# Eight row places instead of up to twelve for the expert rows of the first token block

## The reference, cut to what matters

```python
def peer_ffn(x, w_query, sub_keys, expert_down, expert_up):   # 2 blocks of 128 tokens
    q = (xb @ w_query).reshape(t, 8, 2, 64)
    s = einsum('thpd,hpkd->thpk', q, sub_keys)                # 8 heads, 2 x 128 keys
    top_s, top_i = top_k(s, 16)
    ...                                                       # best 16 of 16 x 16 pairs
    u = expert_down[idx]                                      # one row of 1024 a token and pick
    act = gelu(einsum('td,thkd->thk', xb, u))
    vv = expert_up[idx]
    return einsum('thk,thkd->td', gate * act, vv)
```

## Time and profile before

| | |
|---|---|
| median of 3 runs | 1270.54 us (1269.96 to 1271.0) |
| the profiled execution, own time | 1269.91 us |
| its span, first to last instruction | 1268.2 us |
| mean granted clock of TensorE | 0.98 |
| PE busy | 1172.7 us (92%) |
| DVE busy | 711.9 us (56%) |
| ACT busy | 622.5 us (49%) |
| POOL busy | 752.9 us (59%) |
| bytes by the gathers (queue 0) | 268.45 MB of 381.78 MB |

### The profile page before, as it was taken

One profiled execution on the slowest core, in us unless ns is written; L12 is line 12 of the kernel. 1 busy time (PEld: TensorE's weight loads), 2 busy tenths in 40 slices (PEclk: granted clock), 3 DMA queues, 4 the chain that ended last, 5 costly groups with the idle time before them and its releaser, 6 DMA issues.

```text
span 1268.2 us, 15414 instructions
## 1 busy us (share of the span) xinstructions
PE 1172.7 (92%) x5672; PEld 818.9 (65%) x5672; DVE 711.9 (56%) x1512; ACT 622.5 (49%) x1344; POOL 752.9 (59%) x481
## 2 busy tenths in 40 slices
PE   9999999999998677787799798889999999999998
PEld 8987999965553233333355353443599998888887
DVE  5443135399686675766859678665546533422223
ACT  8586555544434232234424553554654675544442
POOL 7696668645553344554444445454247678788885
PEclk9999999999999898889999999999999999999999
DMA  8553446999999999999999999999524446565542
GB/s 278 193 197 117 149 151 240 370 376 426 425 424 424 424 424 424 424 424 425 424 421 425 424 424 424 416 418 424 218 88 159 134 137 196 167 199 194 181 157 100
DMA packets 121996, 381.78 MB, mean 301 GB/s; under 512 B 8512, under 2 KB 66880, under 8 KB 89152
## 3 DMA queue, kind: packets, MB, share of 16 engines
q0 software_dynamic: 36864, 268.45, 50.7%
q1 hardware_dynamic: 83584, 112.25, 26.7%
q10 hardware_dynamic: 1472, 0.09, 0.1%
HBM read 379.72 MB, written 1.05 MB: 300 GB/s over the span
## 4 chain that ended last, share of the span: by engine, by line
PE 65%; DMA 20%; DVE 7%; ACT 4%; POOL 2%; issue 1%; ACTq 0%; DVEq 0%; POOLq 0%
DMA rows_w<-peer_rows_in,arena 17%; PE ps L1140 15%; PE ps L835 13%; PE ps L864 8%; PE ps L1391 6%; PE ps L1444 4%; PE ps L1395 3%; PE ps L1193 3%; DVE rows_w L2527 3%; PE ps L1344 2%; PE ps L1369 2%; POOL rows_w L778 1%; DMA arena<-peer_rows_in,arena 1%; PE ps L1214 1%; ACT wgt L1770 1%
## 5 line engine op out<-in xcount | busy, mean ns | idle before, releaser
L565 POOL TENSOR_TENSOR w_lo<-ring,w_hi 128x1024 fp32r<-128x1024 f32 x178 | 434.1, 2456 | 160.1 <-ACT w_hi L559 160.0
L1140 PE MATMUL ps<-rows_w,diag 128*128 128x512 f32 x672 | 324.5, 622 | 57.1 <-ACT diag L1779 57.1
L778 POOL DMA_INDIRECT rows_w<-peer_rows_in,arena x168 | 195.4, 1163 | 233.5 <-PE ps L1140 196.9
L1140 PEld LDWEIGHTS ps<-rows_w,diag 128*128 128x128 f32 x672 | 128.1, 199 | 220.4 <-issue 136.6
L2527 DVE CUSTOM_DVE_ANT_0 rows_w<-rows_w,arena 128x1024 f32<-128x1024 f32 x168 | 203.5, 1224 | 103.3 <-DMA rows_w<-peer_rows_in,arena 102.7
L559 ACT ACTIVATE w_hi<-ring 128x1024 fp32r<-128x1024 f32 x178 | 184.1, 1058 | 105.2 <-PE ps L1395 45.5
L1768 ACT ACTIVATE gelu<-dots,rr 128x4 f32<-128x4 f32 (+2 forms) x91 | 27.0, 296 | 318.6 <-DVE dots L2527 318.1
L1140 PE MATMUL ps<-arena,diag 128*128 128x512 f32 x260 | 124.3, 607 | 13.6 <-ACT diag L1779 13.5
L778 POOL DMA_INDIRECT arena<-peer_rows_in,arena x66 | 76.0, 1151 | 59.6 <-PE ps L1140 51.2
L2527 DVE CUSTOM_DVE_ANT_0 arena<-arena 128x1024 f32<-128x1024 f32 x66 | 80.5, 1224 | 37.8 <-DMA arena<-peer_rows_in,arena 37.6
L1140 PEld LDWEIGHTS ps<-arena,diag 128*128 128x128 f32 x260 | 48.5, 194 | 75.0 <-issue 54.1
(11 more groups left out here) (468 smaller groups left out, 2042.6 us busy)
## 6 DMA issues: line engine op xcount, KB each, us to landing
ring<-w_in_in SPq DMA_DIRECT2D x38, 1024.0 KB, 5.2
ring<-w_ffn_gate_in SPq DMA_DIRECT2D x11, 1024.0 KB, 5.3
ring<-w_ffn_up_in SPq DMA_DIRECT2D x11, 1024.0 KB, 5.3
ring<-w_ffn_down_in SPq DMA_DIRECT2D x11, 1024.0 KB, 4.9
ring<-w_out_in SPq DMA_DIRECT2D x8, 1024.0 KB, 7.2
ring<-w_branch_attn_in SPq DMA_DIRECT2D x4, 1024.0 KB, 5.3
ring<-w_branch_mlstm_in SPq DMA_DIRECT2D x4, 1024.0 KB, 5.2
arena<-w_in_in SPq DMA_DIRECT2D x2, 2048.0 KB, 12.1
```

What stands on the lines that cost most here:

```text
L565: pool.tensor_tensor(lo_of(n, u)[:, t, 0:cols], raw_half(n, g)[:, t, 0:cols], hi_of(n, u)[:, t, 0:cols].bitcast(F32), ALU.subtract).then_i ...
L778: pool.indirect_dma_start(pick_row(p, 0, 2 * D), None, a["peer_rows"], bass.IndirectOffsetOnAxis(ap=idx[:, g // PH, j:j + 1], axis=0)).the ...
L1140: ins = pe.matmul(acc[:, c, :], diag[:, p % 4, :], pick_row(p, D + c * CW, CW), start=(p == first), stop=True, skip_group_check=True)
```

## The change

The four places in the ring are added at picks 131, 134, 137 and 140 and no longer at 19, 26, 39 and 52. Up to pick 130 the gathers go round eight places. `TURN_OF_PLACES` grows from 64 to 160, and the swaps that lead to `LAST_PLACES` are made in picks 160 to 255, two passes in a turn and not one. The last turns are the same as before.

```diff
-NEW_AT = {19: 8, 26: 9, 39: 10, 52: 11}
-TURN_OF_PLACES = PICKS // 4
+NEW_AT = {131: 8, 134: 9, 137: 10, 140: 11}
+TURN_OF_PLACES = 160
...
 order = PLACE[-NS:]
 for turn in range((PICKS - TURN_OF_PLACES) // NS):
-    for i in range(turn % 2, NS - 1, 2):
+    for i in (*range(0, NS - 1, 2), *range(1, NS - 1, 2)):
         if LAST_PLACES.index(order[i]) > LAST_PLACES.index(order[i + 1]):
             order[i], order[i + 1] = order[i + 1], order[i]
```

## The result

| | before | after |
|---|---|---|
| median of 4 runs | 1270.45 us | 1289.55 us (1287.44 to 1291.52) |
| ratio, 95% interval | | 1.0148 (1.0136 to 1.0161) |
| the profiled execution, own time | 1269.91 us | 1289.23 us |
| its span | 1268.2 us | 1287.5 us |
| mean granted clock of TensorE | 0.98 | 0.97 |

The change makes the kernel 19.1 us slower. The prediction had the direction and the place, and a fifth of the size: 4.0 us, with a range that ended at 1281.0.

What follows compares the result with a forecast made beforehand. The DMA queue, never empty, was taken to set the pace from first pick to last. The profiled 1269.91 us, plus 4.0 for late groups in picks 64 to 130, plus 0.6 to the median, gave about 1274.4; range 1270.8 to 1281.

Steps and rivals of the forecast that it cites:

- Before pick 64: Stage with two dots at a time: eight places lose nothing, and removing the waits for `query_done` gains nothing.
- The landing into an empty queue: Picks 64 to 130: time from a gather instruction's end to its landing, taken as 5.4 us, between 4.67 and 6.86.
- The sum of a round: Picks 64 to 130, four dots at a time: an undisturbed group just closes, 0.05 us late; 4.0 us lost in all.
- seven long products of the trace before: Seven of 17 groups, picks 64 to 131, have slow first products; the longest cost 1.0 us twice, others 0.6 three times.
- rival 2: Picks 64 to 130: most groups miss through slower landings or fewer full-clock groups; 6.7 to 14 us lost, 1277 to 1285; chance 0.18.
- landings behind the first: Right behind an idle queue landings do not stay at pitch: the first two came 3.4 us apart, not 2.47.
- From pick 131: Four new places refill the queue by four picks, 10 us; block 1's shortest return, 10 picks or 24.7 us, loses nothing.
- What the profile after was to show: In 431 to 600 us: two to five stretches under 424 GB/s, issue to landing 6.5 to 10 us, some late first dots.
- the rate sags in block 1: Sign that would prove the prediction wrong; it expected 413 GB/s in block 1, as before.
- Rival 1: Picks 64 to 130: the loop of eight places closes and nothing changes; 1270.5 to 1272.5 us; chance 0.27.
- Rival 3: In the 1 MB steps a shallower gather queue moves more than 424 GB/s; up to 3 us gained, 1267.5; chance 0.05.
- Rival 4: Another wait than `row_free` holds POOL at eight places, such as unrouted row numbers; no cost, chance counted within Rival 1.

Runs made afterwards that it cites:

- run 1: The changed kernel plus empty TensorE products in idle time: 32 after pick 63, 12 after every fourth pick from 67 to 131; 1278.92 us, ratio 1.0076.
- run 2: The changed kernel plus only the 32 empty TensorE products after pick 63; 1290.05 us, ratio 1.0156.
- run 3: The kernel before the change plus the same empty TensorE products as in run 1; 1270.14 us, ratio 0.9997.
- run 9: The changed kernel with the four ring places added at picks 73 to 76, so one round alone is late; 1273.49 us, ratio 1.0022.
- run 10: The changed kernel with the ring places added at picks 97, 100, 103 and 106, so four late rounds, not eight; 1277.98 us, ratio 1.0058.
- run 5: The changed kernel with a ninth ring place added at pick 19, nine places up to pick 133; 1271.73 us, ratio 1.0010.
- run 14: The changed kernel with a ninth place from pick 19, the others at 136 to 138, one swap pass a turn; 1270.57 us, ratio 1.0002.

## Why the prediction was wrong

**What bounds the kernel, and how a loss comes about: right.** DMA sets the pace, POOL's long waits cost nothing until the queue runs dry, and what is lost stays lost. The prediction named the stage (fours with eight places), the chain (first product, gather, landing) and the first pick that would miss, 72.

**Before pick 64: right.** The landings are 0.7 us behind those of the trace before at pick 0 and 0.1 us ahead of them at pick 71, and 408 and 425 GB/s stand there; the removed waits for `query_done` brought nothing.

**The landing into an empty queue: right in the mean, in part by luck.** It was put at 5.4 us from the instruction's end; eight cases after give 4.5 to 6.9, mean 5.4. But the queue was not empty as at the first gather of all, which took 4.67: at the end of the instruction the gather before still had 0.35 to 1.8 us to its landing. The Trainium skill, page DMA: Bandwidth & Descriptors, section Anatomy of one DMA, would have an estimated 4.4 us from issue for this size; the eight cases took 5.5 to 7.9 and the one gather without any other ahead of it 5.8, so the trace does not agree, and the loop it lets close does not.

**The sum of a round: two of its terms failed.** By the prediction's steps a round without disturbance takes 12.32 us from the first landing to the end of its product (three pitches and 4.91), 0.27 to the gather, 1.80 of instruction and 5.4 to the landing: 19.79. Measured, as the mean of the seven rounds of the table: 15.03, 0.46, 1.28 and 5.50: 22.27.
- *Of the 2.7 us in the first term, 1.76 are the clock.* From the fourth landing to the end of the first product it takes 6.67 us and not 4.91, since the product runs at half clock in every round. The prediction took the seven long products of the trace before as given and let them stand in their old places: five of them lost 3.8 us together, the other twelve groups 0.2. But the idle time of PE is itself an outcome of the change. It asked what an idle PE would do only in rival 2, and there too thought of "fewer groups", not of every round. Runs 1, 2 and 3 show it: without the half clock 9.4 of the 17.1 us come back, the cycle needs no outside push, and with twelve places the clock costs nothing.
- *0.95 are landings behind the first.* The three picks that follow come 8.36 us after the first and not 7.41. The prediction had the row for this (the first two gathers of all landed 3.4 us apart) and said so, and then put 0 for it in the sum: it costed the late pick and went on at pitch from there. Run 9 shows it by itself.

The two together are 2.7 us on a round that was to end within 0.05 us of its time. The gathers' instruction was 0.5 us shorter than assumed, as the late issue mostly misses the dot, and the other two terms were 0.3 longer, which leaves 2.5. Seven rounds of 2.5 us are 17.6; run 10 shows that they add. The two terms cannot be held apart to the last tenth: run 1, with the clock kept, still lost 7.7 us over the same picks, 1.1 a round, where 0.8 would be left without the 1.76.

**Margin.** The prediction argued over 0.05 us at 12 us of work per round (and 5 x 2.47 is 12.35 and not the 12.33 that it used), and gave every term but the landing one value. Runs 5 and 14 (nine places, 2.47 us more, no loss) and the changed kernel (2.5 us short) show how steep it is: one place decides between 0 and 17 us. A sum that ends so near to zero should have had the long products of *every* round as its upper bound: its own 1.0 us for such a product and the 0.93 of its own row for the landings behind (3.4 less 2.47), in eight rounds: 15 us. The upper end given for rival 2 (14 us) came from a landing time alone.

**From pick 131: the queue fills again as said, block 1 loses 2.3 us in the trace.** "10 picks at the shortest, 24.7 us" was set against nothing. The trace before has 15.5 us from the landing to the end of the product at pick 181 and up to 16.9 in the ten picks behind it, and with 6.7 us of gather and landing behind it a loop of ten closes with 1.1 us to spare: near enough to the edge to ask what would lengthen it. After, PE's half clock and DVE's later work (a dot waits up to 6.6 us for it) made it 18.5 us at pick 181 and 19.7 at pick 189, whose places picks 191 and 199 take.

**What the profile after was to show:** GB/s under 424 in two to five stretches: in all of them from 431 to 614. Issue to landing of 6.5 to 10: 5.5 to 12.6, median 9.1. Late first dots at picks 72, 92, 104, 112 and 124: late landings at 72 and then every eighth pick. The clause "I am wrong if the rate sags in block 1" came true (376 GB/s in 745 to 775 us).

**The rivals.** Rival 1 (the loop closes) is refuted for fours and holds for nine places or pairs. Rival 2 (most groups miss, and an idle PE gets its full clock in fewer of them) had the right mechanism, at more than its price. Rival 3 (a shallow queue is faster) has nothing for it: with eight places the stage of pairs moved 425 GB/s. Rival 4 is out.

## What to carry to other kernels

Where a ring of buffers feeds a bound DMA queue, write the round as a sum (landing, use, release, issue, landing) against the number of buffers times the pitch, with the *worst* value of each term, and do not take the clock of the engine in the loop from the old trace: what makes it wait also makes it slow. Near the edge the loss is not the missing tenth of a microsecond but that of a whole cycle, every round; one more buffer, or giving each back sooner (pairs for fours), removes all of it. When places are renumbered, look through every stage for the shortest return, also where nothing was meant to change.

## What the runs showed of the hardware

- **A wait can lock TensorE's clock low.** After 3.9 to 6.7 us without work nine groups of nine started at 1.2 GHz (the records of a product 0.85 us apart and not 0.43, a first product of 3.5 to 3.8 us and not 1.98), and the delay made the next idle time as long. Of the groups that followed after 0 to 1.5 us none did. Between them it went either way: after 3.34 us the first product of pick 180 took 1.98 us before and 3.45 after. The Trainium skill, page TensorE: Matmul & The Clock Gate, section HAM oscillation — how this bites in real kernels, describes a kernel that waits for each slice of data and starts each one slow; the trace agrees, and adds that the delay feeds back into the wait.
- **A gather queue that has run dry is not at its pace again with the first gather.** Landings of 3.20, 2.87 and 2.87 us, then 2.46, with further gathers already queued (run 9); in the changed kernel the second and third landing of a late round came 2.5 to 4.0 us after the one before. In run 9 the spread between the first and the last of the 16 DMA engines to finish a gather falls from 3.0 us to 0.8 in that moment. Why the next ones are slow is left open.
- **The DMA engines run dry one after the other, and before the queue is empty.** The first of them ended pick 71 at 435.04 us and the last at 438.12; the DMA share between 434.5 and 437 us was 0.44.
- **Empty products for the clock are free here** (run 3) and worth 10.6 us with the short loop (run 1), though one more place is worth all of it.
